# When the six early final tiles of a mixture-of-experts stage are gathered, normalised and stored

## What is computed

```
g_idx   = argmax(grp_logits)                      # one of 4 groups per token
top 2 of the 8 experts of that group, softmax weights * p_grp
yb      = (silu(xb @ we_gate[e]) * (xb @ we_up[e])) @ we_down[e]   # D 1024, expert width 256
x       = x + sum over the 2 chosen experts of weight * yb
y       = x * rsqrt(mean(x*x) + eps) * norm_final
```

## Time and profile before

| | us |
|---|---|
| median of 3 runs | 1714.62 (1714.49 to 1716.96) |
| the profiled execution | 1712.31 |
| its span | 1710.6 |
| expert tiles, from the first products to the last result | 1340.4 to 1673.4 |
| last three final tiles, from the last result to the end | 1673.4 to 1710.6 |

### The profile page before, as it was taken

The page is one execution under the profiler, slowest core; times in us unless marked ns, Lnnn a source line. Parts: engine busy times, 40 slices in busy tenths (PEclk is TensorE's granted clock), DMA queues, the critical chain, the costliest instruction groups (busy, mean ns, idle before and its releaser), DMA issues. The chain is left out here.

```text
span 1710.6 us, 29292 instructions
## 1 busy us (share of the span) xinstructions
PE 1558.4 (91%) x12215; PEld 907.1 (53%) x12215; DVE 612.2 (36%) x1304; ACT 371.3 (22%) x716; POOL 338.3 (20%) x401
## 2 busy tenths in 40 slices
PE   7999998999999998999979989999996799898881
PEld 4664464556878887666757655444554232222220
DVE  4203144432266646525523323352145122223232
ACT  3002154442223321121211111121012111212121
POOL 3001156652200000252242200000011412121202
PEclk9999999999999999999989998999998799999995
DMA  6603399988222203432131218236004599999953
GB/s 223 236 20 111 135 338 345 383 312 303 87 89 96 86 25 66 123 100 66 51 64 58 54 46 317 83 101 276 31 38 172 154 395 376 386 381 392 358 210 138
DMA packets 104293, 308.98 MB, mean 181 GB/s; under 512 B 29256, under 2 KB 39688, under 8 KB 93632
## 3 DMA queue, kind: packets, MB, share of 16 engines
q1 hardware_dynamic: 76784, 232.54, 37.4%
q0 software_dynamic: 26080, 70.26, 12.8%
q10 hardware_dynamic: 1296, 4.29, 0.7%
HBM read 258.76 MB, written 56.14 MB: 184 GB/s over the span
## 5 line engine op out<-in xcount | busy, mean ns | idle before, releaser
L1174 PE MATMUL rw_pp<-rows,rw_w 128*128 128x264 f32 x960 | 217.8, 388 | 0.0
L1487 PE MATMUL gate_p<-rows,gate_w 128*128 128x352 f32 x672 | 206.6, 464 | 0.6 <-DMA gate_w<-in_w_in 0.6
L1174 PEld LDWEIGHTS rw_pp<-rows,rw_w 128*128 128x128 f32 x960 | 181.9, 190 | 33.1 <-issue 2.8
L1487 PEld LDWEIGHTS gate_p<-rows,gate_w 128*128 128x128 f32 x672 | 125.8, 190 | 72.2 <-ACT u_rw L1637 5.2
L2275 PE MATMUL x_p<-wgu,rows 128*32 128x512 f32 (+1 forms) x640 | 131.7, 646 | 23.8 <-DMA wgu<-in_we_gu 13.4
L2275 PE MATMUL x_p<-late,rows 128*32 128x512 f32 (+1 forms) x640 | 125.5, 605 | 0.0
L2467 PE MATMUL x_p<-late 128*128 128x512 f32 x256 | 113.1, 595 | 0.0
L1452 POOL DMA_DIRECT2D t_ring<-t_blocks x128 | 69.3, 549 | 140.6 <-DVE tt L1706 135.2
L2293 ACT ACTIVATE rows<-h_p,vec 128x128 f32<-128x128 f32 x96 | 27.4, 367 | 262.5 <-PE h_p L2270 262.5
L2275 PEld LDWEIGHTS x_p<-wgu,rows 128*32 128x32 f32 (+1 forms) x640 | 31.2, 121 | 96.2 <-issue 90.7
L454 POOL DMA_INDIRECT rows<-in_cache_kT,page_index x41 | 42.3, 1031 | 189.2 <-PE fox_b L510 102.4
(11 more groups left out here) (439 smaller groups left out, 2395.8 us busy)
## 6 DMA issues: line engine op xcount, KB each, us to landing
wgu<-in_we_gu SPq DMA_DIRECT2D x16, 2048.0 KB, 14.9
late<-in_we_gu SPq DMA_DIRECT2D x16, 2048.0 KB, 15.4
wd<-in_we_down SPq DMA_DIRECT2D x16, 1024.0 KB, 11.7
late<-in_we_down SPq DMA_DIRECT2D x16, 1024.0 KB, 14.9
rows<-in_cache_kT SPq DMA_DIRECT2D x41, 256.0 KB, 5.2
gate_rows<-u_rw SPq DMA_DIRECT2D x54, 176.0 KB, 1.9
y<-const SPq DMA_DIRECT2D x9, 1024.0 KB, 6.4
rows<-in_cache_v SPq DMA_DIRECT2D x34, 256.0 KB, 8.9
```

What stands on the lines that cost most here:

```text
L1174: mm = pe.matmul(pp[u % 2][:, c, 0:QN], w[:, n % 2, k, :] if n else e.w_first[:, k, :], e.xnT[:, k, at:at + QN], start=(i == 0), stop=(i = ...
L1487: mm = pe.matmul(out[:, 0:GATE_N], gw[:, j % 2, k, :], e.xnT[:, k, at], start=(k == 0), stop=(k == KD - 1))
```

## The change

All six early final tiles are loaded by POOL at tile 21, behind the scatter of tile 20, after a wait for the last gate-up weights of place 3 (`gu_loaded[NW - 1]`), four in the old buffers and two, behind a further wait for tile 21's products, in the gate-up place 0, which tile 21 uses last. Final tile 8 has a buffer over the x rows of tiles 20 and 21; tiles 6 and 7 use buffers 0 and 1 again. Final tiles 0 and 1 are added and squared at t = 22, finished and stored at t = 23; the others follow around and behind the last `out`. `more_rounds` comes behind all nine, and repeats all nine if it runs.

```
-                if at == PER_GROUP - 1 and g:
-                    store(2 * g - 2)
-                    store(2 * g - 1)
+                if t == TILES - 3:
+                    pool.wait_ge(fent_loaded, 32)
+                    pool.wait_ge(gain_loaded, 16)
+                    results_in(TILES * (GR - 1) // GR)
+                    pool.wait_ge(gu_loaded[NW - 1], 16 * NG)
+                    for i in range(4):
+                        load(i)
+                    pool.wait_ge(made_gu, TILES - 2)
+                    for i in range(4, N_EARLY):
+                        load(i)
+                if t == TILES - 1:
+                    store(0)
+                    store(1)
                 pool.wait_ge(y_ready, t + 1)
                 scatter_rows(pool, y[:, t % NW], ent[:, t, 1:2], scattered[t % NW])
                 if t + NW < TILES:
                     gather_rows(pool, x[:, t % NW], ent[:, t + NW, 0:1], gathered[t % NW])
-                if at == 0 and g:
-                    if g == 1: (waits for fent_loaded and gain_loaded)
-                    results_in(t)
-                    load(2 * g - 2)
-                    load(2 * g - 1)
             results_in(TILES)
+            load(N_EARLY)
+            load(N_EARLY + 1)
+            load(N_EARLY + 2)
+            for i in range(2, len(FINALS)):
+                store(i)
...
-            more_rounds(pool, body, repeat)
-            for i in range(N_EARLY, len(FINALS)):
-                load(i)
-            for i in range(N_EARLY, len(FINALS)):
-                store(i)
+            more_rounds(pool, body, repeat, all_stored)
+            all_stored()
```

On DVE, in the loop over t (ACT follows the same places with `deviation`):

```
+                if t == TILES - 1:
+                    finish_tile(0)
+                    finish_tile(1)
                 if t + 1 < TILES:
                     high(t + 1)
                 (wait for silu, multiply)
+                if t == TILES - 2:
+                    total_of(0)
+                    total_of(1)
             keep_turned(TILES - 1)
+            total_of(2)
+            total_of(3)
             out(TILES - 1)
+            total_of(4)
+            total_of(5)
+            for i in range(2, N_EARLY):
+                finish_tile(i)
+            total_of(6)
+            total_of(7)
+            finish_tile(6)
+            total_of(8)
+            finish_tile(7)
+            finish_tile(8)
```

More of the change, by code:

```diff
@@ L2149 @@
 N_EARLY = 2 * (GR - 1)
-PER_GROUP = EPG * R // P
+BUFFER_OF = (0, 1, 2, 3, 4, 5, 0, 1, 6)
+N_BUFFERS = 7
 def stage_experts(e):
@@ L2165, in stage_experts @@
     st = e.steps["dve"]
-    NW, NG, TILES, NFB = 4, NE // 4, NE * R // P, 4
+    NW, NG, TILES = 4, NE // 4, NE * R // P
     NL = NW - EARLY
@@ L2188, in stage_experts @@
                                                                  sem("fent_loaded"), sem("gain_loaded"))
-    f_loaded, f_stored = ([sem(f"f_{n}{b}") for b in range(NFB)] for n in ("loaded", "stored"))
+    f_loaded, f_stored = ([sem(f"f_{n}{b}") for b in range(N_BUFFERS)] for n in ("loaded", "stored"))
     f_sum, f_sq, f_std, f_rstd, f_out = (sem(f"f_{n}") for n in ("sum", "sq", "std", "rstd", "out"))
@@ L2212, in stage_experts @@
         over_x1 = e.x1.rearrange("p t d -> p (t d)")
-        fy = over_x1[:, 0:NFB * 2 * D].rearrange("p (b j d) -> p b j d", b=NFB, j=2)
-        gain = over_x1[:, NFB * 2 * D:(NFB * 2 + 1) * D]
+        pairs_of = lambda v, n: [v[:, b * 2 * D:(b + 1) * 2 * D].rearrange("p (j d) -> p j d", j=2) for b in range(n)]
+        fy = (pairs_of(over_x1, 4) + pairs_of(wgu_early[:, 0].rearrange("p k n -> p (k n)"), 2)
+              + pairs_of(x.rearrange("p u n -> p (u n)"), 1))
+        gain = over_x1[:, 8 * D:9 * D]
         aT = sb("moe_aT", [P, 2, 2, P])
@@ L2256, in gather_results @@
             n = FINALS[i][1]
-            pool.indirect_dma_start(out=fy[0:n, b].rearrange("p j d -> p (j d)"), out_offset=None,
+            pool.indirect_dma_start(out=fy[b][0:n].rearrange("p j d -> p (j d)"), out_offset=None,
                                     in_=e.y2_d.rearrange("(t j) d -> t (j d)", j=2),
@@ L2264, in scatter_results @@
             pool.indirect_dma_start(out=a["y"], out_offset=bass.IndirectOffsetOnAxis(ap=fent[0:n, i, 0:1], axis=0),
-                                    in_=fy[0:n, b, 1], in_offset=None, bounds_check=NTT * P - 1,
+                                    in_=fy[b][0:n, 1], in_offset=None, bounds_check=NTT * P - 1,
                                     oob_is_err=False).then_inc(done, 16)
@@ L2305, in add_results, with more_rounds @@
         def add_results(dve, n, b, done):
-            dve.tensor_tensor(fy[0:n, b, 0], fy[0:n, b, 0], fy[0:n, b, 1], ALU.add).then_inc(done, 1)
-        def more_rounds(eng, body, repeat):
+            dve.tensor_tensor(fy[b][0:n, 0], fy[b][0:n, 0], fy[b][0:n, 1], ALU.add).then_inc(done, 1)
+        def more_rounds(eng, body, repeat, first=lambda: None):
             eng.wait_ge(count_set, 1)
@@ L2312, in more_rounds @@
             with eng.If(longest > R):
+                first()
                 with eng.Fori(1, e.CAP // R) as r:
@@ L2315, in more_rounds @@
                         body(r * NE + ex - NE, ex, r)
-                for i in range(N_EARLY):
+                for i in range(len(FINALS)):
                     repeat(i)
@@ L2405, in load @@
             def load(i):
-                if i >= NFB:
-                    pool.wait_ge(f_stored[i % NFB], 16 * (i // NFB))
-                gather_results(pool, i, i % NFB, f_loaded[i % NFB])
+                b = BUFFER_OF[i]
+                if b in BUFFER_OF[:i]:
+                    pool.wait_ge(f_stored[b], 16)
+                gather_results(pool, i, b, f_loaded[b])
             def store(i):
                 pool.wait_ge(f_out, i + 1)
-                scatter_results(pool, i, i % NFB, f_stored[i % NFB])
+                scatter_results(pool, i, BUFFER_OF[i], f_stored[BUFFER_OF[i]])
             for t in range(TILES):
-                g, at = divmod(t, PER_GROUP)
-                if at == PER_GROUP - 1 and g:
-                    store(2 * g - 2)
-                    store(2 * g - 1)
+                if t == TILES - 3:
[11 more added lines that the diff above has]
+                    store(1)
                 pool.wait_ge(y_ready, t + 1)
@@ L2422, in _, with all_stored @@
                     gather_rows(pool, x[:, t % NW], ent[:, t + NW, 0:1], gathered[t % NW])
-                if at == 0 and g:
-                    if g == 1:
-                        pool.wait_ge(fent_loaded, 32)
-                        pool.wait_ge(gain_loaded, 16)
-                    results_in(t)
-                    load(2 * g - 2)
-                    load(2 * g - 1)
-            results_in(TILES)
+            results_in(TILES)
+            load(N_EARLY)
[3 more added lines that the diff above has]
+                store(i)
+            def all_stored():
+                for b in range(N_BUFFERS):
+                    pool.wait_ge(f_stored[b], 16 * BUFFER_OF.count(b))
             def body(m, ex, r):
@@ L2443, in repeat @@
             def repeat(i):
-                if i == 0:
-                    for b in range(NFB):
-                        pool.wait_ge(f_stored[b], 16 * ((N_EARLY + NFB - 1 - b) // NFB))
                 gather_results(pool, i, 0, again["loaded"])
@@ L2450, in repeat @@
                 pool.wait_ge(again["stored"], 16 * i + 16)
-            more_rounds(pool, body, repeat)
-            for i in range(N_EARLY, len(FINALS)):
-                load(i)
-            for i in range(N_EARLY, len(FINALS)):
-                store(i)
-            for b in range(NFB):
-                pool.wait_ge(f_stored[b], 16 * ((len(FINALS) + NFB - 1 - b) // NFB))
+            more_rounds(pool, body, repeat, all_stored)
+            all_stored()
         @block.tensor
@@ L2627, in deviation @@
                 act_e.wait_ge(sums, k + 1)
-                act_e.activation(fy[0:n, b, 1], fy[0:n, b, 0], ACT.Square, accum_out=fstat[0:n, 0, i:i + 1]).then_inc(squares, 1)
+                act_e.activation(fy[b][0:n, 1], fy[b][0:n, 0], ACT.Square, accum_out=fstat[0:n, 0, i:i + 1]).then_inc(squares, 1)
                 act_e.wait_ge(squares, k + 1)
@@ L2639, in _ @@
                 act_e.activation(act_g[:, t % 2], gu[t % 2][:, 0:DE], ACT.Silu, scale=scale(t)).then_inc(silu, 1)
[L2640 to L2643, removed]
+                if t == TILES - 2:
+                    deviation(0, BUFFER_OF[0], f_sum, f_sq, f_std, 0)
+                    deviation(1, BUFFER_OF[1], f_sum, f_sq, f_std, 1)
+            for i in range(2, len(FINALS)):
+                deviation(i, BUFFER_OF[i], f_sum, f_sq, f_std, i)
             def body(m, ex, r):
@@ L2650, in _ @@
             more_rounds(act_e, body, lambda i: deviation(i, 0, again["sum"], again["sq"], again["std"], i))
-            for i in range(N_EARLY, len(FINALS)):
-                deviation(i, i % NFB, f_sum, f_sq, f_std, i)
         @block.vector
@@ L2821, in total_of @@
             def total_of(i):
```

(9 more changed lines are left out.)

## The result

| | before | after |
|---|---|---|
| median | 1714.55 us (4 runs) | 1686.67 us (4 runs, 1686.28 to 1688.42) |
| ratio | 1 | 0.984, 95% interval 0.9823 to 0.9857 |
| profiled execution, span | 1710.6 us | 1684.6 us |

27.9 us less, where 32 were forecast; 1686.67 lies in the stated range and in the forecast's own (1678 to 1688). Between the two profiled executions the spans differ by 26.0 us. To see where, I divided both traces at the same instructions: silu of tiles 7, 22 and 23, the last `moe_aT` copy, the last `out`, the issue of the first late load, the issue of the last store.

What follows compares the result with a forecast made beforehand. TensorE was taken to bound early expert tiles, DMA engines later ones. Terms -28 + 1 - 1.5 - 0.9 - 1.5 - 1 = -31.9 gave 1680.4 us profiled; with 2.3 for the median 1682.7, stated as 1682, range 1676 to 1695.

Steps and rivals of the forecast that it cites:

- The losses belong to the final tiles (-28): Tiles 7 to 22: moving early final loads and stores out removes the 30.1 us loss, all but 2 us.
- B: Tiles 7 to 22: weights still limit at 375 GB/s, half the losses stay, 15 us; 1695 us, chance 0.13.
- D: Expert tiles: weights are asked for too late, the 30.1 us stay and loads come late; 1722 us, chance 0.06.
- It takes from the rate: Behind early final loads: a load costs its bytes and also lowers the DMA rate, to 320 GB/s from 413.
- The first loads arrive about when they are wanted (+1): Tile 22: DVE's first two final loads land about on time; lateness stops TensorE, bounds 0 and 12 us, 1 taken.
- signs of being right: New profile: loads issued at 1609 to 1618, tile 22's `moe_aT` at most 4 us after silu, among others.
- rival A: Tile 22: the final loads are late, DVE and TensorE wait 12 us; 1694 us, chance 0.11.
- Copy after the last silu (-1.5): Last tile: two finishing operations no longer stand between silu and the `moe_aT` copy, 1.5 us less.
- Last result at the full clock (-0.9): Last result: less TensorE idle before it may keep the full clock, between 0 and -1.8 us, -0.9 taken.
- General path (-1.5): Between last results' landing and first late load: count read and jump go, -1.5 us, bounds 0 and -2.35.
- Tail (-1): After the last `out`: late loads, adds, finishes and four more stores, bounds +4.6 and -2 us, -1 taken.
- Rival C: Behind tile 23: POOL held by a late pair, all finals bunch there, about 12 us; 1694 us, chance 0.04.

Runs made afterwards that it cites:

- first experiment: Kernel before without its six early final tiles (loads, adds, deviations, finishes, stores left out): 1722.54 against 1757.02 us, ratio 0.9798.
- second profile: The changed kernel itself, unaltered, run again on a third chip: 1688.05 us, ratio 0.9826 to the kernel before.
- the trace of the experiment: Kernel before with only the general path's count read and jump moved behind all final tiles: 1716.71 against 1716.49 us, ratio 0.9998.

## Why the prediction was right, and where it was off

- *The losses belong to the final tiles (-28):* right, -29.1; without the tiles 186.72 us are left (first experiment), with the change 186.59. The byte sum came out too low: without final tiles this stretch moved 399 GB/s x 174.2 us = 69.5 MB, not 67.6, so that TensorE's pace asks for about 400 GB/s and not 390, and beside 409 to 413 the DMA engines have some 3% to spare, not 5. It was enough: 1.1 us over TensorE's 185.5 are left, where I let 2 stand. Rivals B and D are out, and the 358 GB/s that the Trainium skill (DMA: Bandwidth & Descriptors, Specifications) gives a core do not bind this case: the core moved 399 over 174 us.
- *"It takes from the rate":* seen in the earlier trace rows, not explained. I read 320 GB/s as what final loads do beside weights. It is what a gather into 112 partitions does. This is the step that the next one failed by.
- *The first loads arrive about when they are wanted (+1):* mis-sized, +5.4 (17.61 - 11.25 = 6.4 in the second profile). I took 320 GB/s for loads and weights together; the stretch ran at 259 and 228, and the gate-up pair took about 4 us longer than the 11.7 us of the earlier trace rows. Two of my signs of being right failed with it: the six loads went out at 1615.86 to 1622.28 instead of 1609 to 1618, and the `moe_aT` of tile 22 was copied 7.4 us after its silu instead of 4. The mechanism, rival A's, happened at under half its price of 12 us. I also left out that a pause of TensorE costs twice: 3.9 us of waiting and some 1.5 us at the lower clock. With 128 partitions the term is 0 (11.25 us), as forecast if "on time".
- *Copy after the last silu (-1.5):* -2.2. I had measured against tile 4's 2.21 us, but there PE makes a part of the next tile's products ahead of the turn; behind the last tile nothing stands there, and the copy can come at 1.52. *Last result at the full clock (-0.9):* all of the -1.8 bound, -1.7.
- *General path (-1.5):* -1.2 at its place, but the trace of the experiment gives a net 0.4; the cost at the end, put at 0, took back the most.
- *Tail (-1):* -0.1, and +1.4 behind the last store. Four more stores are in flight with the late loads: the third landed 9.7 us after its issue against 9.0, and the first add came 5.9 us after the first issue against 5.5. Which part of the +1.4 is the stores and which the general path was not separated; the 0.6 of the experiment is the path's.
- *Rival C* had no share: the last pair landed late (15.5 us), yet the loads still ran beside tile 22.
- +1.4 ahead of tile 7 is untouched by the change; stages before differ by this much and more between executions (the silu of tile 7 comes at 1436.98 to 1448.15 us in the profiles from the other chips than that of the first experiment).
- *Luck in the total:* the profiled execution took 1686.35 us where the sum gave 1680.4, 5.9 more. The median missed by less, 4.7, because I had added the 2.3 us by which the first median stood above the profiled execution, and this time it stood only 0.3 above it. And three gains larger than forecast, of tiles 7 to 22, the copy and the last result (2.5 us together), hid part of the late loads.

**The fastest version:** the changed kernel with 128-row final tiles has the lowest ratio, 0.979: 1682.19 us where the changed one had 1688.05 and the one before 1716.49. That it beats the changed kernel as a whole is not shown, since the intervals overlap. It rests on the first one, two and three groups holding at least 256, 512 and 768 tokens together (the general path repeats the tiles otherwise).

## What to carry to other kernels

Where DMA engines are full, read GB/s beside the share: a share of 1.0 at a quarter or a third less rate than shortly before, as 320 or 259 GB/s here against 413 and 399, can mean that a kind of transfer is expensive, not that there is more of it, and moving it elsewhere moves the price along. Count the partitions of a gather before its bytes; filling it to 128 with rows that nobody reads can be the faster program, as it was here. And when work is moved into a gap, the instruction that first waits for it should not stand ahead of one that the busiest engine needs.

## What the runs showed of the hardware

Indirect gathers of 8 KB rows into 112 or 96 partitions brought all DMA of the core down to 312 to 320 GB/s beside weight traffic and to 228 to 267 with little of it, at a full DMA share; the same gathers into 128 partitions left 402 to 418 (in one trace 361, at a share of 0.93), and 391 with nothing beside them. Repeating 16 rows to fill a 112-row gather shortened a kernel of 1717 us by 17. The Trainium skill (DMA: Bandwidth & Descriptors, The descriptor swizzle) says that in a transfer to 128 partitions each DMA engine writes to one SBUF port of its own; a gather that isn't 128 wide may lose this, which would fit, but no run here shows ports.

After a pause of 3.9 us TensorE's granted clock was 0.72 over the next 5.3 us (1.11 us for a matmul, later 0.59), which cost 1.5 us more. Behind two pauses of 1.1 and 0.5 us it stayed at 1.00; behind two of 1.1 and 2.7 us, before the change, the last result took 5.38 us instead of 3.6.
